# Decoder trunk on one core: prompt attention reordered per branch, cache copies moved into projection, merge in split fp32r

## What is computed

```
P = h @ w_in                              # one projection for all mixers, 67 column tiles of 128
A = gate0 * compressed + gate1 * selected + gate2 * window      # 8 heads, three softmax branches
B = rwkv7(P)                              # recurrence
C = merge of 3 dilated groups by softmax denominators           # 4 heads x 3 groups
m = sum_b sigmoid(gate_b) * (branch_b @ w_br_b)
x = LN(alpha * x + gate_m * (m @ w_o))
x = LN(alpha * x + gate_f * SwiGLU(...))
```

## Time and profile before

| what | us |
|---|---|
| median of 3 runs | 2626.2 (2625.4 to 2628.47) |
| profiled execution, its own time | 2641.51 |
| its span, first to last instruction | 2639.7 |
| prompt attention, first score to last output | 1222.6 to 1588.8 |
| merge, first load to last product | 1959.6 to 2111.3 |

### The profile page before, as it was taken

The page is one execution under the profiler, slowest core; times in us unless marked ns, Lnnn a source line. Parts: engine busy times, 40 slices in busy tenths (PEclk is TensorE's granted clock), DMA queues, the critical chain, the costliest instruction groups (busy, mean ns, idle before and its releaser), DMA issues. The chain is left out here.

```text
span 2639.7 us, 38466 instructions
## 1 busy us (share of the span) xinstructions
PE 2032.3 (77%) x16050; PEld 1728.5 (65%) x16050; DVE 1271.1 (48%) x2016; ACT 520.9 (20%) x1119; POOL 270.6 (10%) x282
## 2 busy tenths in 40 slices
PE   3995798798987897874449881167849939999995
PEld 2985787688887887872225551034348729999994
DVE  3124656765425576722216653546623274444445
ACT  1233333322222332212114440011101000000000
POOL 0000000000004222001114450031300000000000
PEclk7998899899997998965559985588979969999996
DMA  7445222122428666539991001253624013322320
GB/s 239 124 113 130 76 62 74 41 75 62 112 86 267 186 206 160 123 69 347 336 338 55 28 1 39 68 210 109 223 112 168 0 34 91 92 85 74 93 62 34
DMA packets 322362, 317.09 MB, mean 120 GB/s; under 512 B 124781, under 2 KB 278917, under 8 KB 317070
## 3 DMA queue, kind: packets, MB, share of 16 engines
q1 hardware_dynamic: 301486, 196.76, 25.6%
q0 software_dynamic: 18624, 67.64, 7.6%
q10 hardware_dynamic: 2080, 50.23, 5.5%
HBM read 287.10 MB, written 79.71 MB: 139 GB/s over the span
## 5 line engine op out<-in xcount | busy, mean ns | idle before, releaser
L307 PE MATMUL inp_acc<-hh,inp_wh 128*128 128x272 f32 (+1 forms) x1072 | 342.7, 320 | 32.7 <-DVE inp_wl L279 18.5
L307 PE MATMUL inp_acc<-hh,inp_wl 128*128 128x272 f32 (+1 forms) x1072 | 316.5, 295 | 0.0
L307 PE MATMUL inp_acc<-hl,inp_wh 128*128 128x272 f32 (+1 forms) x1072 | 316.0, 295 | 0.0
L307 PEld LDWEIGHTS inp_acc<-hh,inp_wh 128*128 128x128 f32 (+1 forms) x1072 | 207.8, 194 | 55.1 <-issue 27.9
L279 DVE TENSOR_TENSOR inp_wl<-inp_w,inp_wh 128x1024 fp32r<-128x1024 f32 (+1 forms) x67 | 81.2, 1212 | 269.3 <-ACT inp_wh L459 268.8
L307 PEld LDWEIGHTS inp_acc<-hl,inp_wh 128*128 128x128 f32 (+1 forms) x1072 | 208.5, 194 | 3.4 <-issue 3.0
L307 PEld LDWEIGHTS inp_acc<-hh,inp_wl 128*128 128x128 f32 (+1 forms) x1072 | 207.6, 194 | 0.5
L288 PE MATMUL ffn_acc<-ffn_hh,ffn_wh 128*128 128x272 f32 x704 | 146.9, 290 | 36.3 <-DVE ffn_wl L279 36.3
L1348 PE MATMUL cmp_pH<-cmp_RTh,cmp_w1h 128*128 128x256 f32 (+1 forms) x576 | 173.4, 301 | 0.3 <-DVE cmp_RTl L279 0.3
L1348 PE MATMUL cmp_pH<-cmp_RTl,cmp_w1h 128*128 128x256 f32 (+1 forms) x576 | 170.3, 296 | 0.0
L1348 PE MATMUL cmp_pH<-cmp_RTh,cmp_w1l 128*128 128x256 f32 (+1 forms) x576 | 170.0, 295 | 0.0
(11 more groups left out here) (446 smaller groups left out, 3953.8 us busy)
## 6 DMA issues: line engine op xcount, KB each, us to landing
inp_w<-in_w_in_dram SPq DMA_DIRECT2D x66, 512.0 KB, 4.4
out_dram<-in_cache_dil_dram ACTq DMA_DIRECT2D x1, 32704.0 KB, 161.8
ffn_w<-in_w_ffn_dram SPq DMA_DIRECT2D x60, 512.0 KB, 3.9
sdi_kv<-in_cache_dil_dram SPq DMA_DIRECT2D x192, 86.0 KB
pat_wada<-in_w_ada_dram SPq DMA_DIRECT2D x16, 1024.0 KB, 27.8
PT<-inp_o SPq DMA_DIRECT2D x58, 272.0 KB, 2.2
ada_wada<-in_w_ada_dram SPq DMA_DIRECT2D x8, 1024.0 KB, 9.2
out_dram<-in_cache_dil_dram ACTq DMA_DIRECT2D x1, 8128.0 KB, 51.3
```

What stands on the lines that cost most here:

```text
L307: i = pe.matmul(out, l, r, start=(first and n == 0), stop=(last and n == 2))
```

## The change

Three parts.

**Cache copies.** `shift_caches` becomes a generator on GpSimd's queue in projection. The copies are cut into 92 pieces (64 of dil2, 16 of dil1, 8 of win, 4 of dil0); each waits until projection has finished a given tile, from tile 15 to tile 64.

**Prompt attention.** Scores wait per branch for the bias pass on their bank. Bias passes and maxima are separate, in the order bias 0, bias 1, maximum 0, bias 2, maximum 1, maximum 2. Exponents are released per branch. GpSimd's multiplication is gone: unweighted exponents are transposed. Value products have tokens on the partitions (stationary pT, moving values of 64 columns), one accumulation per branch side by side in a bank of pO, and VectorE combines the three with the weights into oc. Each pair of units is transposed back once by TensorE and copied by ScalarE (`out`). pX has two banks in place of three, filled in the order of `items`. The modulation steps stand at turns 4 to 11 and 17 to 24.

**Merge.** Every product is made of three fp32r matmuls. Weights come in 16 column blocks through three buffers; ScalarE makes the high parts, VectorE the low parts; the activations and the merged tiles are split too.

```diff
-def shift_caches(sp, a, copied):
+def shift_caches(eng, proj, a, copied):
+    pieces = cache_pieces(a)
+    first, last = 15, len(proj.tiles) - 2
+    for i, (dst, src) in enumerate(pieces):
+        n = first + i * (last - first) // len(pieces)
+        yield proj.at(n)
+        eng.wait_ge(proj.done, 2 * n)
+        eng.dma_start(dst, src).then_inc(copied, 16)
...
-                weave(mix.pool(pool))
+                weave(mix.pool(pool), shift_caches(pool, proj, a, m["copied"]))
...
-    mod_at = [3 + 2 * l for l in range(KD)] + [24 + 2 * l for l in range(KD)]
+    mod_at = [4 + l for l in range(KD)] + [17 + l for l in range(KD)]
+    items = []
+    for i in range(NU + 7):
+        if 0 <= i - 2 < NU:
+            items += [(i - 2, b) for b in range(3)]
+        if 0 <= i - 6 < NU and (i - 6) % 2:
+            items.append((i - 6, "out"))
+    item = {x: n for n, x in enumerate(items)}
...
-        pX = ps("pX", [P, 3, 512])
-        pO = ps("pO", [P, 2, 256])
+        pX = ps("pX", [P, 2, 512])
+        pO = ps("pO", [P, 2, 512])
...
+                def score(u, b):
                     if u:
-                        pe.wait_ge(sx, u)
+                        pe.wait_ge(sr, 3 * (u - 1) + b + 1)
+                    q, k, _, n, _, _, _ = branch(u, b)
+                    pe.matmul(pS[:, b, 0:n], q, k, start=True, stop=True).then_inc(sc, 1)
+                def turn(u, b):
+                    w = item[u, b]
+                    pe.wait_ge(ex, 3 * u + b + 1)
+                    if w >= 2:
+                        pe.wait_ge(tk, w - 1)
...
                 def values(u):
                     if u >= 2:
                         pe.wait_ge(oe, u - 1)
+                    for b in range(3):
+                        pe.wait_ge(tk, item[u, b] + 1)
                         vs = branch(u, b)[4]
                         for k, v in enumerate(vs):
+                            i = pe.matmul(pO[:, u % 2, b * HD:(b + 1) * HD], pT[0:v.shape[0], u % 2, b, k * P:(k + 1) * P], v,
+                                          start=(k == 0), stop=(k == len(vs) - 1))
...
+                    for b in range(3):
+                        if i < NU:
+                            score(i, b)
+                        if 2 <= i < NU + 2:
+                            turn(i - 2, b)
+                    if 3 <= i < NU + 3:
                         values(i - 3)
+                    if (i - 6, "out") in item:
+                        out(i - 6)
...
             def _(act):
                 act.wait_ge(loaded, NLOAD)
-                shift_caches(act, a, m["copied"])
...
                     if i < NU:
-                        act.wait_ge(sx, i + 1)
                         for b in range(3):
+                            act.wait_ge(sx, 3 * i + b + 1)
...
-                    if i >= 2:
+                    if 2 <= i < NU + 2:
                         u = i - 2
                         for b in range(3):
+                            w = item[u, b]
+                            act.wait_ge(tr, w + 1)
+                            nc.scalar.activation(pT[0:r, u % 2, b, 0:c], pX[0:r, w % 2, 0:c], ACT.Copy).then_inc(tk, 1)
...
-            @block.gpsimd
-            def _(pool):
-                for u in range(NU):
-                    pool.wait_ge(wt, u + 1)
-                    for b in range(3):
-                        n = branch(u, b)[3]
-                        pool.tensor_scalar(s[:, u % 3, b, 0:n], s[:, u % 3, b, 0:n], st[:, u % 4, 2, b:b + 1], None, ALU.mult).then_inc(sd, 1)
...
+                def combine(u):
+                    c(dve.tensor_scalar(o, x(0), w(0), None, ALU.mult))
+                    c(dve.scalar_tensor_tensor(o, x(1), w(1), o, ALU.mult, ALU.add))
+                    dve.scalar_tensor_tensor(o, x(2), w(2), o, ALU.mult, ALU.add).then_inc(oe, 1)
...
+                        biased(i, 0)
+                        biased(i, 1)
+                        top(i, 0)
+                        biased(i, 2)
+                        top(i, 1)
+                        top(i, 2)
...
-                            for h in range(2):
-                                i = pe.matmul(acc[:, w % 4, h, 0:HN], wb[:, at + k, n * P:(n + 1) * P],
-                                              m[src][:, k, h * HN:(h + 1) * HN], start=(k == 0), stop=(k == nk - 1))
+                            i = split_product(pe, acc[:, u % 4], (wh[:, n % 2, at + k], wl[:, n % 2, at + k]),
+                                              (xh[:, at + k], xl[:, at + k]), k == 0, k == nk - 1)
```

More of the change, by code:

```diff
@@ L1771, in merge, with arrived @@
         acc = ps("acc", [P, 4, 2, 512])
-        mT = sb("mT", [P, KD, NT])
-        loaded, xl, wol, sig, done, used, ch, out, oused = (sem(s) for s in ("loaded", "xl", "wol", "sig", "done", "used", "ch", "out", "oused"))
+        xloaded, xhigh, xlow, whigh, wlow, sig, done, used, ch, out, oused, merged = (
+            sem(s) for s in ("xl", "xhigh", "xlow", "whigh", "wlow", "sig", "done", "used", "ch", "out", "oused", "merged"))
         gl = [sem(f"g{i}") for i in range(2)]
+        loaded = [sem(f"w{i}") for i in range(3)]
+        def arrived(i):
+            return 16 * sum(3 if j < KD else 1 for j in range(i % 3, i + 1, 3))
+        chunks = lambda i: NB if i < KD else KD
         with nc.Block() as block:
@@ L1820, in _ @@
                     for k in range(KD):
-                        for h in range(2):
-                            i = pe.matmul(acc[:, n % 4, h, 0:HN], wo[:, k, n * P:(n + 1) * P], mT[:, k, h * HN:(h + 1) * HN],
-                                          start=(k == 0), stop=(k == KD - 1))
+                        if n == 0:
+                            pe.wait_ge(merged, k + 1)
+                        i = split_product(pe, acc[:, n % 4], (wh[:, n % 2, k], wl[:, n % 2, k]), (mh[:, k], ml[:, k]), k == 0, k == KD - 1)
                     i.then_inc(out, 1)
@@ L2014, in branch @@
                     dist[:, 1 + b, (3 - qt + k0) * P:SEQ])
+        others = lambda u: len([x for x in range(u) if units[x][1] == "C"])
         with nc.Block() as block:
@@ L2044, in _ @@
                 pe.wait_ge(qs, 2)
-                def scores(u):
+                def score(u, b):
                     if u:
-                        pe.wait_ge(sx, u)
-                    for b in range(3):
-                        q, k, _, n, _, _, _ = branch(u, b)
-                        i = pe.matmul(pS[:, b, 0:n], q, k, start=True, stop=True)
-                    i.then_inc(sc, 1)
-                def turn(u):
-                    for b in range(3):
-                        w = 3 * u + b
-                        pe.wait_ge(sd, w + 1)
-                        if w >= 3:
-                            pe.wait_ge(tk, w - 2)
-                        n = branch(u, b)[3]
-                        for k in range(-(-n // P)):
-                            c = min(P, n - k * P)
-                            i = pe.transpose(pX[0:c, w % 3, k * P:(k + 1) * P], s[:, u % 3, b, k * P:k * P + c], m["ident"][:, :])
-                        i.then_inc(tr, 1)
+                        pe.wait_ge(sr, 3 * (u - 1) + b + 1)
+                    q, k, _, n, _, _, _ = branch(u, b)
+                    pe.matmul(pS[:, b, 0:n], q, k, start=True, stop=True).then_inc(sc, 1)
@@ new lines, in turn @@
+                def turn(u, b):
[3 more added lines that the diff above has]
+                        pe.wait_ge(tk, w - 1)
+                    n = branch(u, b)[3]
+                    for k in range(-(-n // P)):
+                        c = min(P, n - k * P)
+                        i = pe.transpose(pX[0:c, w % 2, k * P:(k + 1) * P], s[:, u % 3, b, k * P:k * P + c], m["ident"][:, :])
+                    i.then_inc(tr, 1)
@@ L2075, in values, with out @@
                         for k, v in enumerate(vs):
-                            i = pe.matmul(o, v, pT[0:v.shape[0], u % 2, b, k * P:(k + 1) * P],
-                                          start=(b == 1 and k == 0), stop=(b == 0 and k == len(vs) - 1))
+                            i = pe.matmul(pO[:, u % 2, b * HD:(b + 1) * HD], pT[0:v.shape[0], u % 2, b, k * P:(k + 1) * P], v,
+                                          start=(k == 0), stop=(k == len(vs) - 1))
                     i.then_inc(pv, 1)
-                for i in range(NU + 3):
+                def out(u):
+                    w = item[u, "out"]
+                    pe.wait_ge(oe, u + 1)
+                    pe.wait_ge(tk, w - 1)
+                    pe.transpose(pX[:, w % 2, 0:P], oc[:, u // 2 % 3, :], m["ident"][:, :]).then_inc(tr, 1)
@@ L2192, in _ @@
                     if i >= 4:
-                        output(i - 4)
+                        combine(i - 4)
 def sample_nsa(nc, a, m):
@@ L2718, in build, with finish @@
             feed_forward(nc, a, m)
-        finish(nc, m)
-def finish(nc, m):
+        finish(nc, a, m)
+def finish(nc, a, m):
     with nc.Block() as block:
```

210 lines of the change are left out of this document (128 added, 82 removed).

## The result

The changed kernel takes 2785.7 us in the median of four runs (2783.3 to 2792.1), the kernel before 2627.0 beside it: ratio 1.061, interval 1.059 to 1.063. It is slower by 159 us, 85 us more than predicted and 11 us above the range. The profiled execution has a span of 2790.1 us and its own time is 2792.05, 150.5 above that of before.

The account below looks back on a forecast made before the run. Three stages mattered: projection with TensorE busy, attention slowed by DMA waits and half clock, merge on TensorE. Attention +100, projection +4, merge -29 made +75 on 2641.5, carried over to 2701 us; range 2600 to 2775.

Parts of the forecast that it names:

- The loop through the ring: Prompt attention: with two pX banks the third turn waits for ScalarE's first copy, a 1.9 to 3.7 us pause per unit.
- The prices: Attention: TensorE's work plus pause per unit, summed to 340 us at full clock and 544 at half.
- The step that failed: Attention clock: A tiles 1 and 2 at half, the rest midway; 466 us, +100, bounds -26 and +178.
- rival (b): Attention at half clock throughout, +178; 2779 us in all; chance 0.09.
- rival (a): Attention at nearly full clock from tile 2 on, about 360 us; 2595 us in all, faster; chance 0.19.
- Projection: Cache copies paced through projection are covered by weight prefetch; +4 us, between 0 and +25.
- rival (c): Copies disturb projection, token stores and recurrence loads land later; +25 on the forecast, 2722 us; chance 0.07.
- Merge: Merge: fp32r products save 23.6 us, an earlier start 7, splits cost some back; -29 us (-20 to -33).
- The vanished waits: Attention: moving the copies off ScalarE's queue removes 69.0 us of TensorE waits for pat_wada.
- the milder case: Attention between 385 and 430 us, between the forecast and nearly full clock; chance 0.12.
- (d): The ring does not end the attention loop, units run at TensorE's sum; about 250 us, 2485 in all; chance 0.03.

Follow-up runs that it names:

- copies first with wide values: Changed kernel with ScalarE's pT copies ahead of the exponents and value matmuls moving 128 columns, not 64; 2500.0 us, 0.952 of the kernel before; repeated, 2488.7 us.
- copies first: Changed kernel with ScalarE's three pT copies of unit i-2 issued ahead of the exponents of unit i; median 2670.3 us, one run 2608.0.
- three banks: Changed kernel with three pX banks and two pS banks, 2679.5 us, ratio 1.015; with pT copies ahead of exponents and 128-column values too, 2512.4 us, 0.955.
- the old attention without the copies: Kernel before with cache copies moved into projection and the new merge, prompt attention as before; 2544.4 us, ratio 0.964.
- the one profile of a start at full clock: Changed kernel with pT copies ahead of exponents, 64-column values and some 90 useless matmuls before the first unit; median 2669.3 us, one run 2603.4.
- paced: Kernel with pT copies ahead of exponents and 128-column values, its 92 cache pieces issued by GpSimd across attention units instead of projection; 2475.7 us, 0.944.
- issued at once: Kernel with pT copies ahead of exponents and 128-column values, its four whole cache copies issued by ScalarE at the start of attention; 2619.7 us, 0.998.

## Why the prediction was wrong, point by point

**The loop through the ring** held: the third turn waits in every unit, 3.4 us on average by the row of the weight load (161.6 in 47), 2.6 by that of the transpose (118.5 in 46), and either a third bank or copies ahead of the exponents takes 124 to 127 us out of attention.

**The prices** held at half clock. Half clock throughout was put at 544 us, and it came out at 550.0. Units of the last A tile were put at 14.2 without a modulation step; those of the trace are 14.5 us apart (1521.9, 1536.4, 1551.0, 1565.5). In the third tile 11.5 and a modulation step of 1.94, together 13.4, were forecast; its two halves have 12.95 and 13.81. TensorE's own work at half clock, 2 x 192 for the units and 31 for the steps, 416, against 422.6 to 425.6 with the pause taken out. The value matmul at 0.11 a record held too. At full clock the sum was too low, which half clock hid: a unit of the last A tile without a pause was put at 5.4 us, and in copies first with wide values such units are 6.3 and 6.2 us apart (1365.05, 1371.39, 1377.62), some 0.1 of it due to the width. The term is the 0.7 us for seven changes between kinds of matmul, the lower end of the range given for them; these units have about 1.4 left for it.

**The step that failed** is the clock: "so I take tiles 1 and 2 of A at half clock (8 x 14.9 = 119), the rest midway between its 246 and 394 (320)". It was half clock to the end: attention +183.8 in place of +100. Of the miss on the profiled execution, 75.5 us (150.5 against 75), attention is 83.8 and projection 11.8; merge gives back 1.7 and the untouched stages 18.5. It was rival (b), at 2779 forecast and given 0.09. The reason for the 1.00 expected in the late tiles was that they have 1.00 today; but today's values move 128 columns and the new ones 64, in the same 0.11 us. I priced that edit as "no gain" in time and left it out of the argument on the clock. One of the arguments was misread too: rival (a) has the clock fall during the DMA waits, but the earlier trace rows has 0.50 in the 37.9 us before them and 0.56 in the stretch with them. The runs show the weight of the width, with the two causes crossed (attention, us, and the clock in it without its first and last 30 us):

| | 64 moving columns | 128 moving columns |
|---|---|---|
| pause in each unit | 550.0, 0.50 | 497.0, 0.53 to 0.75 |
| pause filled by matmuls of 256 columns | 372.4, 0.86 to 1.00 | not run |
| no pause (copies first) | 422.6, 0.50 | 249.0, 1.00 |
| no pause (three banks; on the right with copies first) | 425.6, 0.50 | 274.0, 0.79 to 1.00 |

Either alone keeps most of attention near half clock. Taking out the pause gives 127 us, widening the values 53, both 301. What in the narrow stream lowers the clock, no run shows.

**Projection** was mis-sized: +4 with "its length unchanged" in mind, and it grew by 15.8 in the profiled execution, within the bounds of 0 to 25. DMA was at 0.50 where I expected 0.6. The prefetch did not cover all: the weight loads land in 7.2 us in place of 4.3, and the waits for them on ScalarE rose from 6.9 us to 24.9, nearly all of the rise in the last tiles, after 725 us. The rows for them (us, times), and TensorE's wait behind:

```profile
  DMA inp_w<-in_w_in_dram: 24.9, 5
...
  PE inp_acc L307: 25.2, 3
...
DMA to landing us min/median/max: 2.8/7.2/10.6
```

TensorE had most of that wait before as well, at the start of projection; the trace before:

```profile
PE inp_tb L422 <- ACT inp_tok L467: 21.5, 1, 21.5
...
PE inp_acc L307 <- DVE inp_wl L279: 18.5, 1, 18.5
```

So the weights account for 6.7 us on TensorE. Another 4.5 are the wait of the first of these rows, which is 26.0 us in the changed kernel: ScalarE stands before it for a store of tokens, 28.2 us in place of 23.6, which is what rival (c) names. The other 4 to 5 us stay open.

**Merge** held: start 7.7 us (8 forecast), phases 64.0 and 49.3 (64 and 49), together -30.7 against -29. TensorE stayed the bound. The 23.6 us of the forecast were less than its prices give (0.461 less 0.373, times 288, is 25.3); the two phases gave 22.6.

**The vanished waits** held: none for pat_wada, and the old attention without the copies takes 284.4 us, 81.8 less than before: the 69.0 us and a clock that is up earlier. That the waits had kept it down is argued.

**The rivals.** (a) and the milder case died with the clock. (c) is half true, 15.8 of its 25, and part of it by the way it names. (d), about 250 us of attention at TensorE's sum, is what the kernel does once two lines of it are other: 249.0. That the number meets is luck: the forecast's own prices give 192 and 17, 209 us, at full clock, and the changes between kinds cost more than that. The chance of a faster kernel was put at 0.20 where (a) and (d) alone have 0.22; and the 51.1 us for eight units before are 6.4 each, not 6.5. Neither enters the time.

## What to carry to other kernels

Price an edit of a matmul's shape twice: for its time, and for what it makes of the clock; here halving the moving columns gained almost no time of its own and cost 174 us of attention through the clock (422.6 against 249.0, profiled runs). Before a ring is made smaller, write out for each bank which instruction of the same turn frees it and what stands ahead of that in its engine's queue. And if a rival differs from the forecast only by the clock, and the new loop has a pause in each turn that the old one lacks, give the half clock more than the 0.09 of a tail; with narrow values it was 0.50 throughout, with wide ones 0.53 to 0.75.

## What the runs showed that was not expected

A TensorE that has work in 50.00 of 50 us stays at 1.2 GHz for over 350 us (three banks, copies first), and in the one profile of a start at full clock it is back at 1.2 GHz within 4 us of the first score. Useless matmuls, up to 2.9 us a unit, take 178 us off attention. Moving 128 columns of which 64 are never read costs about 0.1 us a unit (records 0.11 us apart in both forms) and, with the pause gone too, brings the full clock for most of attention. 47 MB of copies in 249 us beside 16 MB of w_ada, with DMA at 0.99 to 1.02 in places, lengthen attention by nothing when paced (248.8 against 252.1) and by 133 us when issued at once (385.5).
